# An encoder block with 32 routed experts: tokens reordered by their last expert, part of the gate products placed among the experts

## Time and profile before

| | |
|---|---|
| Median of 3 runs | 514.59 us |
| Lowest, highest | 512.97, 515.79 us |
| Profiled execution | span 512.3 us; its device time is not listed apart, the three runs lie 0.7 to 3.5 us above this span |
| PE busy | 477.8 us, 93% |
| DVE, ACT, POOL busy | 232.3, 169.8, 149.9 us |
| Moved by DMA | 144.73 MB, mean 283 GB/s |
| Mean granted TensorE clock | 0.987 |

### The profile page before, as it was taken

How to read it: one execution, slowest core, us unless ns; L and a number is a source line. 1 busy time by engine, 2 the same in 40 slices (tenths; PEclk the granted TensorE clock), 3 DMA queues, 4 the chain that set the end, 5 groups by cost and what they waited for, 6 DMA issues and landing times.

```text
span 512.3 us, 7264 instructions
## 1 busy us (share of the span) xinstructions
PE 477.8 (93%) x2718; PEld 264.5 (52%) x2718; DVE 232.3 (45%) x683; ACT 169.8 (33%) x283; POOL 149.9 (29%) x136
## 2 busy tenths in 40 slices
PE   3799999999999999989999999987999997999993
PEld 3355555744854457655555555543454553444441
DVE  2899948999233258642222222220211211565525
ACT  6633576547442333111111111120122111214454
POOL 1079999614100001222222222220121210003250
PEclk9999999999999999999999999997999998999998
DMA  8874300399499986899999999999999996990022
GB/s 299 145 202 93 70 0 2 125 155 168 156 357 412 421 339 221 316 391 421 419 418 419 418 414 417 419 418 420 420 421 419 416 406 228 399 371 2 0 82 82
DMA packets 60140, 144.73 MB, mean 283 GB/s; under 512 B 27587, under 2 KB 36839, under 8 KB 47817
## 3 DMA queue, kind: packets, MB, share of 16 engines
q1 hardware_dynamic: 54504, 133.92, 71.0%
q0 software_dynamic: 5328, 10.31, 5.3%
q10 hardware_dynamic: 272, 0.04, 0.0%
HBM read 138.17 MB, written 14.19 MB: 297 GB/s over the span
## 4 chain that ended last, share of the span: by engine, by line
PE 69%; DMA 18%; SPq 5%; DVE 3%; issue 2%; ACT 2%; POOL 0%; DVEq 0%; POOLq 0%
PE bank L1653 63%; DMA ring<-in_exp_w_up_dram 6%; DMA big<-in_exp_w_up_dram 6%; DMA moe<-v_d,gidx_all 4%; SPq L388 3%; DMA pairs_d<-moe,sidx_all 2%; PE bank L2059 1%; PE bank L1753 1%; SPq L364 1%; PE bank L1743 1%; PE bank L2078 1%; PE bank L1916 1%; PE bank L2176 1%; DVE moe L922 1%; SPq L393 1%
## 5 line engine op out<-in xcount | busy, mean ns | idle before, releaser
L1653 PE MATMUL bank<-ring,moe 128*64 128x256 f32 (+2 forms) x848 | 112.0, 410 | 3.7 <-DMA ring<-in_exp_w_up_dram 3.2
L1653 PEld LDWEIGHTS bank<-ring,moe 128*64 128x64 f32 x848 | 60.8, 140 | 40.7 <-issue 15.6
L1579 POOL DMA_INDIRECT pairs_d<-moe,sidx_all x32 | 31.8, 993 | 155.0 <-PE bank L2059 78.9
L922 DVE TENSOR_TENSOR vrow<-moe,bank 64x128 f32<-64x128 f32 x64 | 18.7, 291 | 118.3 <-ACT moe L821 117.3
L1653 PE MATMUL bank<-ut,big 128*128 128x512 f32 x128 | 57.7, 597 | 1.2 <-ACT ut L562 1.2
L821 ACT ACTIVATE moe<-bank 64x256 f32<-64x256 f32 x32 | 12.1, 377 | 138.2 <-PE bank L1653 138.2
L550 ACT ACTIVATE moe<-bank 128x512 f32<-128x512 f32 (+1 forms) x65 | 36.5, 582 | 60.6 <-PE bank L1653 50.5
L1653 PE MATMUL bank<-ring,ut 128*128 128x512 f32 x128 | 55.7, 593 | 0.4 <-DVE ut L922 0.4
L1653 PE MATMUL bank<-big,moe 128*64 128x256 f32 (+1 forms) x264 | 43.2, 440 | 3.0 <-DMA big<-in_exp_w_up_dram 2.6
L922 DVE TENSOR_TENSOR ring<-ring,bank 128x64 f32<-128x64 f32 (+1 forms) x142 | 39.5, 278 | 2.8
L1653 PEld LDWEIGHTS bank<-ring,ut 128*128 128x128 f32 x128 | 24.0, 190 | 29.3 <-issue 29.3
(11 more groups left out here) (198 smaller groups left out, 616.8 us busy)
## 6 DMA issues: line engine op xcount, KB each, us to landing
ring<-in_exp_w_gate_dram SPq DMA_DIRECT2D x19, 1024.0 KB, 23.8
ring<-in_exp_w_down_dram SPq DMA_DIRECT2D x18, 1024.0 KB, 26.9
ring<-in_exp_w_up_dram SPq DMA_DIRECT2D x17, 1024.0 KB, 20.2
big<-in_exp_w_up_dram SPq DMA_DIRECT2D x7, 1024.0 KB, 20.1
big<-in_exp_w_down_dram SPq DMA_DIRECT2D x7, 1024.0 KB, 18.2
big<-in_exp_w_gate_dram SPq DMA_DIRECT2D x6, 1024.0 KB, 20.6
ut<-in_exp_w_up_dram SPq DMA_DIRECT2D x4, 1024.0 KB, 24.0
h<-in_exp_w_down_dram SPq DMA_DIRECT2D x4, 1024.0 KB, 23.0
```

What stands on the lines that cost most here:

```text
L922: return dve.tensor_tensor(o, a, b, op)
L1579: pool.indirect_dma_start(pairs, bass.IndirectOffsetOnAxis(ap=index, axis=0), at(moe, ALL, M_Y + k * 512, [[1, 512]]), None, bounds_check= ...
L1653: return pe.matmul(o, a, b, start=start, stop=stop, skip_group_check=loose)
```

## The change

Once the experts are running, DVE, PE and POOL sort the tokens by the larger of their two expert numbers (`sort_masks`, `sort_positions`, `sort_values`, `sort_out` in steps 2 to 7; small operations). All that comes behind the experts is then done in sorted tiles: tile 0 has the 128 tokens that are done first.

- SP writes zeros over all of `pairs_d` (4 MiB, 2 KB a packet) behind the load of the second half of W_out; the piece loads wait for its end. The early scatter of zero rows goes; scatters stop at expert 28, and 29, 30 and 31 (`LASTS`) are added by `combined`, into the last tile alone.
- Rows of v (`rows_h`), of the pairs (`rows_pairs`) and of p are fetched by POOL through indirect DMAs by the sorted index `perm_i`, the first two tiles during the experts: h at steps 14 and 27, pairs at 14 and 22 behind a wait for all scatters so far (`scattered`), p at 18. If fewer than 128, 256, 384 tokens have their last expert by 14, 22, 28 (`EARLY`), `flag` is set so that the general loop runs.
- W_gate is loaded by SP between the pieces, in two halves of 2 MiB, in front of pieces 52 and 61, and W_proj in front of 67 (before: p and W_proj in front of 56). `RETIRE` takes slots out for this: the piece whose slot a piece takes is 22 pieces back up to piece 51, 15 at piece 61, 11 at 70, 9 at 80 and 7 from 87 on (before: 22, then 20 and, from 78 on, 18).
- Among the experts: transposes of sorted tiles 0 and 1 at steps 19 and 27 (`th_step`), gate products n = 0, 1, 2 at steps 20, 22, 28 (`gate_step`), whose raw results DVE copies out (`raw_out`). `p_rows` goes from step 19 to 21, `proj` from 21, 23, 25, 27 to 23, 25, 29, 30.
- The tail has gate products 3 to 7, in an order written out by hand on each engine (below). The norm of tiles 0 to 2 waits for all three (`root4(0, NA, ...)`). The output is scattered by POOL through indirect DMAs.

```diff
...
+        LASTS = (NE - 3, NE - 2, NE - 1)
+        EARLY = (14, 22, NE - 4)
...
         PP_BANK = (0, 6)
-        P_ROWS, P_PROJ = 19, (21, 23, 25, 27)
+        P_ROWS, P_PROJ = 21, (23, 25, 29, 30)
...
         ORDER = [(0, 0), (0, 1)] + [x for e in range(NE - 1) for x in ((e + 1, 0), (e + 1, 1), (e, 2))] + [(NE - 1, 2)]
+        RETIRE = {8: 30, 9: 30, 0: 36, 1: 36, 10: 46, 11: 46, 16: 52, 17: 52, 18: 36, 12: 34, 21: 43, 13: 58, 19: 70,
+                  14: 76, 15: 76}
         SPOT, AFTER = list(range(NPIECE)), [None] * NPIECE
         for q in range(3 * NE):
-            kept = (SPOT[q] in (10, 11) and q >= NPIECE) or (SPOT[q] in (16, 17) and q >= 52)
+            kept = q >= RETIRE.get(SPOT[q], 3 * NE)
...
+        def consumed(eng, slots):
+            for q in sorted(LAST_IN[i] for i in slots):
+                e, k = ORDER[q]
+                eng.wait_ge(gu_ps if k < 2 else dn_ps, e + 1)
...
+            sp.wait_ge(blank_set, 1)
+            sp.dma_start(dr(pairs_d, 0, [[16 * 512, P], [512, 16], [1, 512]]), at(ut, ALL, 0, [[0, 16], [1, 512]])
+                         ).then_inc(zs_stored, 16)
...
+            sp.wait_ge(zs_stored, 16 * (GB * NB + 1))
             weights(sp, 20)
...
+            def load_gate(half):
+                sp.dma_start(at(ring, ALL, E_WPLE[half], [[512, KC], [1, 512]]),
+                             dr(A["ple_gate_w"], half * 512, [[DM, P], [P * DM, KC], [1, 512]])
+                             ).then_inc((ld_wple, ld_wple1)[half], 16)
...
+            between = ((8, 9), lambda: load_gate(0)), ((0, 1), lambda: load_gate(1)), ((10,), load_proj)
             for p in range(NPIECE, 3 * NE):
+                for slots, load in between:
+                    if AFTER[p - 1] is None or not AFTER[p - 1] < max(LAST_IN[i] for i in slots) < AFTER[p]:
+                        continue
+                    consumed(sp, slots)
+                    load()
                 e, k = ORDER[AFTER[p]]
-                if AFTER[p] == 34:
...
-            def load_h(t):
-                sp.dma_start(at(h, ALL, t * DM, [[1, DM]]), dr(v_d, t * P * DM, [[DM, P], [1, DM]])).then_inc(ld_pairs[t], 16)
...
-            sp.wait_ge(gu_ps, NE - 5)
-            sp.wait_ge(dn_ps, NE - 6)
-            load_h(0)
-            sp.wait_ge(gu_ps, NE - 1)
-            load_gate(0, 0, 4, ld_wple)
-            sp.wait_ge(moe_done, 1)
-            sp.wait_ge(gu_ps, NE)
-            load_pairs(0)
-            sp.wait_ge(dn_ps, NE - 1)
-            load_gate(0, 4, 4, ld_wple)
-            load_h(1)
...
+            def h_scale(t):
+                act.wait_ge(v_moved[t // 2], 64)
+                act.wait_ge(sort_done, PERM_SET)
+                hv = at(h, ALL, t * DM, [[1, DM]])
+                act.activation(hv, hv, ACT.Copy, scale=pv(t, 1)).then_inc(v_done, 1)
...
                                accum_out=at(small, ALL, col, [[1, 1]])).then_inc(ss_done, 1)
-            for t in range(NT - 1):
-                norm3(t)
-            for t in range(NT - 1):
-                sigmoid(2 * t)
-                sigmoid(2 * t + 1)
-                warm(2 + t)
-                if t == 0:
...
-            sigmoid(2 * NT - 1)
-            warm(2 + NT)
-            square_half(2 * NT - 1, S_SS4 + NT - 1)
-            act.wait_ge(ss_done, 4 * NT + 1)
+            root3(0, 2, 2)
+            square3(2)
+            root3(2, 1, 3)
+            act.wait_ge(comb, 4 * NT + 2)
+            act.activation(junk_at(NA), at(h, ALL, NA * DM, [[1, DM]]), ACT.Square,
+                           accum_out=at(small, ALL, S_SS3 + NA, [[1, 1]])).then_inc(ss_done, 1)
+            root3(NA, 1, 4)
+            for n in range(4):
+                sigmoid(n)
+            square4(0)
+            square4(1)
+            sigmoid(4)
+            sigmoid(5)
+            square4(2)
+            warm(2)
+            root4(0, NA, NA, S_EPS)
...
+            def add_rows(t, n, k, done):
+                hv = at(h, ALL, t * DM + n * 512, [[1, 512]])
+                dve.scalar_tensor_tensor(hv, at(big, ALL, t * PIECE + k * DM + n * 512, [[1, 512]]), pv(t, 2 + k), hv,
+                                         ALU.mult, ALU.add).then_inc(done, 1)
+            def combine(t):
+                if t < NA:
+                    dve.wait_ge(ld_pairs, 16 * (t + 1))
+                else:
+                    dve.wait_ge(v_moved[1], 80)
+                dve.wait_ge(v_done, H_SCALED + t + 1)
+                for n in range(2):
+                    add_rows(t, n, 0, comb)
+                for n in range(2):
+                    dve.wait_ge(comb, 4 * t + n + 1)
+                    add_rows(t, n, 1, comb)
...
+            def raw_out(n):
+                dve.wait_ge(gate_ps, n + 1)
+                dve.tensor_copy(sg_at(n), bank[GATE_BANK[n]][:, :]).then_inc(gate_in, 1)
...
-            for t in range(NT - 1):
-                gate(2 * t)
-                if t + 2 < NT:
-                    turned_g_ple(t + 2)
-                gate(2 * t + 1)
-                if t == 0:
-                    combine(NT - 1)
-                    inverse(S_RS3 + NT - 1, 1, NT + ROOT3[NT - 1])
-                else:
-                    final(t - 1)
-            gate(2 * NT - 2)
...
-            dve.wait_ge(ss_done, 4 * NT)
+            turned_out(2, turned_ps, TH_PS + 6, ut_done)
+            combine(NA)
+            combine_last()
+            inverse_of(S_RS3, 2, ROOT3 + 1)
+            dve.wait_ge(ld_fin, 32)
+            for n in range(4):
+                gate(n)
+            turned_out(NA, turned_ps, TH_PS + 8, ut_done)
+            inverse_of(S_RS3 + 2, 1, ROOT3 + 2)
+            gate(4)
+            gate(5)
+            inverse_of(S_RS3 + NA, 1, ROOT3 + 3)
+            inverse_of(S_RS4, NA, ROOT4 + 1)
+            scaled(0, 0, DM).then_inc(fin_done, 1)
+            gate(6)
+            gated_sum(6)
+            scaled(1, 0, DM).then_inc(fin_done, 1)
+            scaled(2, 0, DM).then_inc(fin_done, 1)
+            dve.wait_ge(ss_done, SS4 + NA + 1)
...
-            inverse(S_RS4 + NT - 1, 1, NT + ROOT4[NT - 1])
+            gate(7)
+            gated_sum(7)
+            inverse_of(S_RS4 + NA, 1, ROOT4 + 2)
...
+            def sorted_rows(o, source, t, done):
+                pool.indirect_dma_start(o, None, source, bass.IndirectOffsetOnAxis(ap=perm_i[:, t:t + 1], axis=0),
+                                        bounds_check=T - 1, oob_is_err=False).then_inc(done, 16)
...
+            def scattered(n):
+                for k in range(YBUF):
+                    pool.wait_ge(ys_stored[k], 16 * len(range(k, n, YBUF)))
+            for e in range(NE - LX):
                 if e % 2 == 0 and 0 < e and e // 2 + XBUF < NE // 2:
                     gather(e // 2 + XBUF)
                 scatter(e)
-            for k in range(YBUF):
-                pool.wait_ge(ys_stored[k], 16 * len(range(k, NE - 2, YBUF)) + 32 * (k == 2))
+                if e in EARLY[:2]:
+                    t = EARLY.index(e)
+                    if t == 0:
...
+                        consumed(pool, (18, 12))
+                        rows_h(0, v_moved[0])
+                        rows_h(1, v_moved[0])
+                    else:
+                        consumed(pool, (13,))
+                    scattered(e + 1)
+                    least(pool, ld_pairs, 16 * t)
+                    rows_pairs(t, ld_pairs)
+                if e == 18:
+                    consumed(pool, (11,))
+                    pool.wait_ge(v_moved[0], 64)
+                    for t in range(NT):
+                        sorted_rows(at(ring, ALL, E_PIN + t * DPLE, [[1, DPLE]]), dr(A["p"], 0, [[DPLE, T], [1, DPLE]]), t, v_moved[0])
+                if e == 27:
+                    consumed(pool, (19,))
+                    rows_h(2, v_moved[1])
+                    rows_h(3, v_moved[1])
+            scattered(NE - LX)
...
+            def store(o, index, source, rows):
+                pool.indirect_dma_start(o, bass.IndirectOffsetOnAxis(ap=index, axis=0), source, None,
+                                        bounds_check=rows - 1, oob_is_err=False).then_inc(stored, 16)
...
+                gated_sum(n)
+            for t in range(NA):
+                pool.wait_ge(fin_done, t + 1)
+                store(out_d, perm_i[:, t:t + 1], at(ring, ALL, E_O + t * DM, [[1, DM]]), T)
+            for n in range(2):
+                pool.wait_ge(fin_done, NT + n)
+                store(dr(out_d, 0, [[512, 2 * T], [1, 512]]), perm_h[:, n:n + 1],
+                      at(ring, ALL, E_O + NA * DM + n * 512, [[1, 512]]), 2 * T)
...
+                parts = (n * CAP, (n + 1) * CAP)
+                to, off = SLOTS[i]
+                return mm(bank[CMB_BANK[n]][:, :], at(to, parts, off, [[1, P]]),
+                          at(moe, parts, M_Y + x % YBUF * 512, [[1, 512]]), i == 0, i == LX - 1, True)
...
+            def th_step(t):
+                pe.wait_ge(comb, 4 * (t + 1))
+                turned_h(t, turned_ps)
...
-            pe.wait_ge(slot_done, 1)
```

(17 more changed lines are left out.)

476 lines of the change are left out of this document (304 added, 172 removed).

## The result

The changed kernel takes 525.09 us (median of 4 runs, 524.37 to 527.44), the kernel before on the same chip 514.39. The ratio is 1.0217, 95% interval 1.0191 to 1.0242: slower by 2.2%, 10.7 us. The interval lies clear of no change and reaches a little under 2%. The forecast was 520.0 us, range 505 to 528, slower with 0.60.

What follows compares the result with a forecast made beforehand. Loads and PE were taken as two close bounds of the expert stage, the moved loads deciding. D 461.9 plus tail and store 55.9 gave a span of 517.8, with 2.3 to the median 520.0 us; range 505 to 528.

Steps and rivals of the forecast that it cites:

- D: End of the expert stage, when `dn_sb` reaches its end value 32: 437.56 us before, forecast 461.9, 24.3 later.
- The full stage: Slices 18 to 32, 231 to 423 us: DMA runs at 406 to 421 GB/s without a gap, PE nearly always busy.
- the loads hide: Rival for the expert stage: moved loads don't hold PE up, D = 447.6, time 505.8 us; chance 0.14.
- Piece 69 decides: Up half of expert 23: lands at 375.6, PE ready at 361.8, so PE idles some 13 us in steps 15 to 22.
- PE idle over 8 us for weights before mark 23: Sign to look for in the expert stage: PE's waits for weight DMAs before mark 23 exceed 8 us in all.
- A product put there is free: Steps 15 to 22: a gate product, 6.87 us, fits PE's idle time of some 13 us; that time is lost anyway.
- The sort: Steps 2 to 8: some 30 small DVE operations and six small PE products, costed at nothing.
- The later marks: Experts after mark 23 at 387.8: mark 24 at 397.1, 30 at 449.3, with a 0.6 us wait for piece 87.
- The tail: Behind D: PE ends at D + 38.0, bias of n = 7 at D + 45.5, behind POOL, ACT and DVE; D + 51.1 in all.
- PE sets the tail: Rival for the tail: POOL keeps up, D + 48.1, time 512.3 us, no change; chance 0.17.
- The store: Indirect DMA at the end: 4 us from the second half's issue and 0.5 us to the end, giving D + 55.9.
- The zeros: 4.19 MB zero write before the pieces: 10.5 us, covered by 14.9 us of free engine time, costed at nothing.

Runs made afterwards that it cites:

- both_gather_weights: Changed kernel with x fetches 10 and 14 issued ahead of the large sorted fetches and only an eighth of W_gate loaded: 519.6 us, ratio to before 1.0112.
- gather_first: Changed kernel with x fetches 10 and 14 issued by POOL ahead of the large sorted fetches: 528.1 us, ratio to before 1.0273.
- gate_weights_eighth: Changed kernel loading only an eighth of W_gate, 3.67 MB less, so its gate products aren't the reference's: 521.8 us, ratio to before 1.0151.
- tail_order: Changed kernel with ACT's sums of squares later and DVE's biases of n = 6 and 7 earlier in the tail: 520.8 us, ratio to before 1.0133.
- tail_both: Changed kernel with tail_order's orders, and n = 3 and tile 2's transposes in front of `combined`: 520.2 us, ratio to before 1.0133.
- mended: tail_both with earlier gathers and h fetch, `h_scale(0)` at step 17, W_gate's second half, W_proj and product n = 1 later: 525.9 us, ratio to before 1.0229.

## Why the prediction was right, step by step

The time and its sign were right, but D, the larger part of the sum, came out right by luck: in the step that gave it two errors nearly cancelled. Two terms behind it were mis-sized. From the predicted span of 517.8 to 525.8 it is +0.9 (D) + 3.8 (D to the last `scaled`) + 3.3 (from there to the end). The medians are closer, 525.1 for 520.0: each time lies 1.6 or 1.7 us over its span, but the profiled execution was 2.3 over its kernel's median, and that of before somewhat under. The late start of `combined` (below) is seen in this one execution; the three others had spans 2.0 to 3.1 shorter, and whether they have it isn't known.

- **The full stage.** "This stage has no room for loads" held. With 3.67 MB less the stage is shorter by 2.8 with nothing else changed, by 6.5 with the gather early (both_gather_weights against gather_first), and by 8.4 with the products gone. With D at 462.81 for 447.6 the rival "the loads hide" falls.
- **Piece 69 decides.** This step failed. I looked at one piece alone. By my own sum piece 63 was to land at 359.1 (353.03 − 8.27 + 14.3), and 104 us of PE work follow it to mark 31, 20.5 of them up to `gu_step(23)`: that gives 379.6 for my 375.6. It landed at 355.33, 3.7 earlier than the sum. The two errors, the wrong piece and a stream reckoned too late, left 0.3 us at `gu_step(23)`. Not "PE idle over 8 us for weights before mark 23" either: 1.79 for weights, 6.82 for the gather, 1.34 for DVE. I named the late gather and said that at step 18 its lateness falls into idle time. gather_first bears that out. But that the idle time was then seen as a wait for the gather, not for the weights, I hadn't thought of.
- **"A product put there is free."** Right beside W_gate's bytes, 1.9 of 20.6 us. Not a price of the product by itself: without these bytes it is 7.4.
- **The sort.** I had put it at nothing. From mark 2 to mark 17 PE needs 94.0 us (229.30 to 323.28), for 91.8 before (230.01 to 321.82): steps 3, 6 and 8 are longer by 0.9, 1.2 and 0.6, and step 4 shorter by 0.6. That the sort's PE products are the cause is argued from their place in steps 3 and 6; no run leaves the sort out.
- **ACT's wait for h** was no term of mine. It costs 1.34 in front of step 18, 4.53 once the gather comes early, and 3.87 with less weight besides.
- **The later marks.** 24 to 30 stand at 397.70 to 450.14, for 397.1 to 449.3: the durations taken from the earlier trace rows give mark 23 to mark 30 as 61.5 us, measured 61.8. Piece 87's wait was 0.27 for 0.6.
- **The tail.** The chain from D to the last `scaled` was 51.1. In gate_weights_eighth and both_gather_weights, whose tails are untouched, it is 51.0. In the changed kernel PE began `combined` 2.24 us late behind a stretch put down to issue, and at a lower clock (granted 0.57 from 464 to 468 us; eight products took 3.60, for the 1.99 of tail_order): 3.9 more. The named order, POOL and ACT behind DVE's wait in `turned_out(2)`, held, with `square4(1)` in front of `sigmoid(4)` as said (495.49, and POOL's gap of 1.78 behind it). "PE sets the tail" falls; tail_both shows what it would have been worth.
- **The store.** Landing was 2.7, not 4, and by the Trainium skill's fit ("DMA: Bandwidth & Descriptors", section "Anatomy of one DMA — SWDGE (gpsimd) path"), which gave 2.6, the trace agrees. The term that failed is the 0.5 us behind it: 4.0. The second half's issue, at 519.09, also came 1.1 later behind the last `scaled` than I had put it (1.4 for 0.3), since it stands behind the first's.
- **The zeros.** Cost nothing, as forecast. Their DMA landed 25.1 us after its issue (116.78 to 141.9). The load of W_out in front of it landed at 130.8, which leaves 11.1 us for the zeros, where I had reckoned 10.5; what of my cover of 14.9 us was left isn't known.

Where did the gain go? Mark 17 of the kernel before is this row of its timeline of PE:

```profile
321.82 0.33 PE L2078 MATMUL bank<-cst,vrow 128*128 128x128 f32 x1
```

From before to after, in spans: mark 17 to D 139.5 for 115.7 (+23.8), D to the last `scaled` 54.9 for 72.3 (−17.4), the end 8.1 for 2.5 (+5.6), the front +1.5 (mark 2 stands 0.7 earlier, and from there to mark 17 it is 2.2 longer). In sum +13.5. The tail gave what was meant. Of the stage's +23.8, W_gate's bytes and the products together are 10.3; the rest, waits for gather and weights that hide each other, transposes and the other moved bytes, wasn't taken apart further.

## What to carry to other kernels

Work put into an engine's idle time brings operands that need room in the stream of loads: in this stage, where PE and the stream run level, 20.6 us of products alone cost 7.4 us, 3.67 MB of their weights alone 8.4, and both 10.3. Where two lines run level, a wait in one is only worth what the other leaves; take both away in one kernel before you price either, and check every piece of a stream against its consumer, not the one that was late before. A product belongs in front of the wait that it is to fill: behind it, as in mended, it is added to the wait.
